# Mixture-of-experts stage of a two-layer hybrid step: the raw weight ring turns unbroken over the fixed rounds, the 64-slot tile's down product moves behind its next gate product, and the 128-slot rounds split their weights one unit further ahead

## The reference

```python
N_EXP = 8
TOP_K = 2
D_FF_E = 1408

def moe_swiglu(h, router, w_gu, w_down):
    ...
    logits = (hf @ router).astype(jnp.float32)
    top_v, top_i = lax.top_k(logits, TOP_K)
    wts = jax.nn.softmax(top_v, axis=-1)
    ...
    g, u = jnp.split(jnp.einsum('nd,edf->nef', hf, w_gu), 2, axis=-1)
    act = jax.nn.silu(g) * u * gate[..., None].astype(h.dtype)
    return jnp.einsum('nef,efd->nd', act, w_down).reshape(B, T, D)
```

## Time and profile before

| | before |
|---|---|
| time, median of 3 runs | 2532.23 us (2530.74 to 2536.68) |
| the profiled execution's own time | 2524.19 us |
| its span, first to last instruction | 2522.5 us |
| PE busy | 2192.5 us, 87% of the span |
| DVE busy | 1326.5 us, 53% |
| ACT busy | 935.1 us, 37% |
| HBM traffic | 134 GB/s over the span |

### The profile page before, as it was taken

One profiled execution on the slowest core, in us unless ns is written; L12 is line 12 of the kernel. 1 busy time (PEld: TensorE's weight loads), 2 busy tenths in 40 slices (PEclk: granted clock), 3 DMA queues, 4 the chain that ended last, 5 costly groups with the idle time before them and its releaser, 6 DMA issues. The chain is left out here.

```text
span 2522.5 us, 41799 instructions
## 1 busy us (share of the span) xinstructions
PE 2192.5 (87%) x17111; PEld 1845.0 (73%) x17111; DVE 1326.5 (53%) x1865; ACT 935.1 (37%) x1462; POOL 425.2 (17%) x459
## 2 busy tenths in 40 slices
PE   5998597999899999998994878988699898899993
PEld 4987365668899999998983665677467666787882
DVE  5566666654422222235565676644355655655546
ACT  4333024653422112114331246633344544544443
POOL 0036332541000000000064334610100000000002
PEclk8999798999899999998997899999799999999996
DMA  6331773923222232212315710021766877846645
GB/s 225 87 93 34 168 239 107 343 88 101 62 73 63 80 83 68 58 52 66 89 30 122 196 62 1 1 65 44 272 208 210 291 242 255 283 158 225 217 147 193
DMA packets 370847, 340.75 MB, mean 135 GB/s; under 512 B 90593, under 2 KB 339887, under 8 KB 369647
## 3 DMA queue, kind: packets, MB, share of 16 engines
q1 hardware_dynamic: 354447, 279.26, 36.4%
q10 hardware_dynamic: 11520, 41.95, 5.1%
q0 software_dynamic: 4704, 17.04, 1.7%
HBM read 287.42 MB, written 50.79 MB: 134 GB/s over the span
## 5 line engine op out<-in xcount | busy, mean ns | idle before, releaser
L2839 DVE TENSOR_TENSOR w_lo<-w_raw,w_hi 128x2048 fp32r<-128x2048 f32 (+1 forms) x138 | 306.5, 2228 | 156.8 <-ACT w_hi L2677 156.4
L2677 ACT CAST w_hi<-w_raw 128x2048 fp32r<-128x2048 f32 (+1 forms) x138 | 255.0, 1856 | 47.9 <-PE ps L2609 29.3
L2577 PE MATMUL ps<-w_hi,h_hi 128*128 128x512 f32 (+1 forms) x528 | 203.5, 385 | 20.6 <-DVE w_lo L2839 20.6
L2577 PE MATMUL ps<-w_hi,h_lo 128*128 128x512 f32 (+1 forms) x528 | 198.2, 375 | 0.0
L2577 PE MATMUL ps<-w_lo,h_hi 128*128 128x512 f32 (+1 forms) x528 | 198.1, 375 | 0.0
L3121 PE MATMUL ps<-ffn_h_hi,w_hi_ffn 128*128 128x320 f32 x704 | 161.5, 311 | 5.5 <-DVE ffn_h_lo L379 4.2
L3121 PE MATMUL ps<-ffn_h_lo,w_hi_ffn 128*128 128x320 f32 x704 | 161.3, 310 | 0.0
L3121 PE MATMUL ps<-ffn_h_hi,w_lo_ffn 128*128 128x320 f32 x704 | 161.3, 310 | 0.0
L1869 DVE TENSOR_REDUCE tm<-ps 128x1 f32<-128x768 f32 (+1 forms) x140 | 111.7, 818 | 49.7 <-PE ps L1765 31.6
L2577 PEld LDWEIGHTS ps<-w_hi,h_hi 128*128 128x128 f32 x528 | 100.4, 190 | 49.8 <-issue 22.6
L571 PE MATMUL ps<-w_hi_in,h_hi 128*128 128x454 f32 x320 | 122.4, 382 | 4.8 <-DVE w_lo_in L153 3.3
(11 more groups left out here) (478 smaller groups left out, 5155.1 us busy)
## 6 DMA issues: line engine op xcount, KB each, us to landing
w_raw<-in_moe_w_gu SPq DMA_DIRECT2D x186, 512.0 KB, 5.1
w_raw<-in_moe_w_down SPq DMA_DIRECT2D x41, 1024.0 KB, 7.3
G_decay<-in_ada_w ACTq DMA_DIRECT2D x54, 512.0 KB, 4.6
w_ahead<-in_ffn_w_gu SPq DMA_DIRECT2D x44, 512.0 KB, 5.3
slots_h<-tm SPq DMA_DIRECT2D x14, 1024.0 KB, 10.7
slots_y<-tm SPq DMA_DIRECT2D x13, 1024.0 KB, 11.6
w_ahead<-in_ffn_w_down SPq DMA_DIRECT2D x16, 704.0 KB, 4.7
oA<-in_ada_w ACTq DMA_DIRECT2D x20, 512.0 KB, 4.8
```

Source lines behind the costliest of these rows:

```text
L2577: mm = pe.matmul(ps[:, bank, 0:2 * columns(u)], x[:, k, tile * P:(tile + 1) * P], gate_up(wt, u, k), start=(k == 0 and n == 0), stop=(k == ...
L2677: act.copy(part(whi, n), raw_piece(n)).then_inc(s["w_hi"], 1)
L2839: dve.tensor_tensor(part(wlo, n), raw_piece(n), part(whi, n).bitcast(F32), ALU.subtract).then_inc(s["w_lo"], 1)
```

## The change

Three things are altered, all of them in the rounds.

1. **Places in the ring.** Over the fixed rounds, a piece's place is its number counted from the first round, modulo 6, and no longer from the start of its own round. With 17 pieces a round, before, the first pieces of the next round waited for pieces 12 to 16 and 11; now they wait for 11 to 16 in turn. In the loop the turn is still broken at each round (`holder`, `raw_slot`, `landed`).
2. **The small tile's down product.** Unit u-1's is now issued right behind unit u's small gate product. It raises a semaphore of its own, `few_dn`, which SP waits for; `dn` is raised by tile 0's down product. The last unit's goes in the order small tile, then tile 0.
3. **Splits in 128 rounds.** The two gate pieces of unit 1 are split at the start of the round, and behind the `gate` of unit u both gate pieces of unit u+2; `take` follows, then the split of d(u). Piece d5 is split after the last of these. The loads' order is unchanged.

```diff
-        raw_slot = [n % RAW for n in range(NP)]
...
+        loop_slot = [(NP * STATIC + n) % RAW for n in range(NP)]
...
+            def splits_of(c):
+
+                if c != 128:
+                    return list(range(NP))
+                order_ = [at("g", 0, 0), at("g", 0, 1), at("g", 1, 0), at("g", 1, 1)]
+                for u in range(NU - 1):
+                    order_ += next_pieces(u)
+                    order_ += [at("d", u, 0)]
+                order_ += [at("d", NU - 1, 0)]
+                return order_
...
+            def holder(r, n, ahead):
+
+                if not ahead:
+                    return n - RAW
+                if isinstance(r, int):
+                    return NP + n - RAW
+                return max(m for m in range(NP) if loop_slot[m] == loop_slot[n])
...
                     def down(r, u, tile):
                         c = size(r)
                         pe.wait_ge(s["a_lo"], unit_done(r, u))
-                        pe.wait_ge(s["w_lo"], count("pieces", r, at("d", u) + 1))
+                        pe.wait_ge(s["w_lo"], rank(r, at("d", u)))
...
-                        if tile == max(tiles_of(c)):
+                        if few(c, tile):
+                            mm.then_inc(s["few_dn"], 1)
+                        elif tile == (0 if c == 192 else max(tiles_of(c))):
                             mm.then_inc(s["dn"], 1)
...
                             for tile in order:
                                 multiply(r, u, tile)
+                                if u and few(c, tile):
+                                    down(r, u - 1, tile)
...
-                            if u and c == 192:
-                                down(r, u - 1, 1)
-                        for tile in range(len(order)):
+                        for tile in order:
                             down(r, NU - 1, tile)
...
+                        if c == 128:
+                            split(r, at("g", 1, 0))
+                            split(r, at("g", 1, 1))
                         for u in range(NU - 1):
                             gate(r, u, order[0])
+                            if c == 128:
+                                for n in next_pieces(u):
+                                    split(r, n)
+                                take(r, u, 0)
+                                split(r, at("d", u))
+                                continue
                             split(r, 3 * u + 2)
...
+                        if c == 128:
+                            split(r, at("d", NU - 1))
                         gate(r, NU - 1, order[0])
                         split(r, 0, 1)
```

More of the change, by code:

```diff
@@ L2276, in experts @@
             names = (self.NORM + " w_in io zeroed moved_pool mm_t lg_t mm chain diff expd chosen count turned_t h_tok slots table scattered issued "
-                     "blk_in h_turned h_hi h_lo w_hi w_lo gu silu prod a_turned a_hi a_lo dn y_act y_dve y_store y_free "
+                     "blk_in h_turned h_hi h_lo w_hi w_lo gu silu prod a_turned a_hi a_lo dn few_dn y_act y_dve y_store y_free "
                      + " ".join(f"raw{q}" for q in range(RAW)))
@@ L2418, in wait_raw_free @@
             def wait_raw_free(eng, r, n):
[L2420 to L2425, removed]
+                kind, u, _ = ORDER[n]
+                eng.wait_ge(s["w_hi"], rank(r, n))
+                eng.wait_ge(s["w_lo"], rank(r, n))
+                if size(r) == 192:
                     if kind == "g":
-                        eng.wait_ge(s["gu"], tile_count(r - 1 if n < 0 else r, u, 1))
+                        eng.wait_ge(s["gu"], tile_count(r, u, 1))
                     else:
-                        eng.wait_ge(s["dn"], count("units", r - 1 if n < 0 else r, u + 1))
+                        eng.wait_ge(s["few_dn"], count("few", r, u + 1))
             with stage(nc, names) as (block, s):
@@ L2673, in split @@
                     def split(r, n, ahead=0):
[L2674 to L2675 removed]
+                        act.wait_ge(s[f"raw{raw_slot(r, n, ahead)}"], landed(r, n, ahead))
                         wait_used(act, r, hl_before[n] + NP * ahead)
[L2677 removed]
+                        act.copy(part(whi, n), raw_piece(r, n, ahead)).then_inc(s["w_hi"], 1)
                     def gate(r, u, tile):
@@ L2837, in split @@
                     def split(r, n, ahead=0):
-                        dve.wait_ge(s["w_hi"], count("pieces", r, NP * ahead + n + 1))
-                        dve.tensor_tensor(part(wlo, n), raw_piece(n), part(whi, n).bitcast(F32), ALU.subtract).then_inc(s["w_lo"], 1)
+                        dve.wait_ge(s["w_hi"], rank(r, n, ahead))
+                        dve.tensor_tensor(part(wlo, n), raw_piece(r, n, ahead), part(whi, n).bitcast(F32), ALU.subtract).then_inc(s["w_lo"], 1)
                     def gate(r, u, tile):
@@ L2941, in _ @@
                     for q in range(RAW):
-                        pool.wait_ge(s[f"raw{q}"], per_round[q] * rounds + (per_round[q] * STATIC + landed[q]))
+                        pool.wait_ge(s[f"raw{q}"], loop_total[q] * rounds + (static_total[q] + incs[loop_slot.index(q)]))
     def combine(self, l, pos, w):
```

74 lines of the change are left out of this document (46 added, 28 removed).

## The result

The changed kernel took 2545.94 us in the median of 5 runs (2541.0 to 2556.53), the kernel before 2532.23 (2525.2 to 2536.68). The ratio is 1.0074, with a 95% interval of 1.0052 to 1.0095: slower by 13 to 24 us, where 7.5 was forecast. The direction was right, the size was not. The time itself lies in the range of 2529 to 2550.

The account below looks back on a forecast made before the run. PE bounds the 192 rounds; 128 rounds, where PE waits mostly for DVE's w_lo, have something to give. 22.5 us lost less 15 gained is 7.5 slower: 2532.23 + 7.5 = 2539.7 us, range 2529 to 2550 (8 in 10).

Parts of the forecast that it names:

- What bounds the kernel: Fixed rounds: PE busy 79.7 of 82 us in a 192 round, 52 to 53 of 66 to 67 in a 128 round.
- the 256 rounds at nothing: 256 rounds: they keep their order and ring, so their cost was put at zero.
- PE stands longer in the 192 rounds: 192 rounds: new waits at the moved small down product, for w_lo or a_lo, lose 7.0 + 7.75 + 7.75 = 22.5 us.
- PE stands less in the 128 rounds: 128 rounds: earlier splits shorten PE's waits, giving 3.7 us in round three and 3.4 in round five.
- the clock: 128 rounds and behind round three: with no wait over 2.4 us left, the clock stays up, giving 2.6 + 1.7 + 1.6 us.
- the rest: 128 rounds: 0.6 us each from gate products no longer standing still midway, and the gain of 14.2 rounded up to 15.
- the bound of 27: 192 rounds: upper bound of the loss in three rounds, 3 x 9 us; the lower bound was nothing.
- the part on the loads: 128 rounds: at 352 GB/s g31 lands at about 19 us, wanted at 16.2, which takes 1.5 us back.
- the sign of being wrong: 128 rounds: waits of ACT for DMA of more than 3 us would say that the loads bind.
- Faster as a rival: 128 rounds run at PE's pace alone, giving 34 us, less 22.5 lost in the 192 rounds: 2521 us; chance 0.15.
- The rival of over 11 us slower: Waits of 2.0 to 2.5 us in 192 and 128 rounds each halve the clock, 1.7 us each time: 2551; chance 0.16.
- The ring does nothing as a rival: Ring: loads had slack, so its turn gives nothing; inside the forecast, 1 to 3 us of the gain; no chance given.

Follow-up runs that it names:

- e3: Changed kernel, small down product waiting only for its raw piece and its own tile's activation; ratio 0.9966 to the kernel before.
- e9: Changed kernel, next round's block loaded behind the round's first four weight loads; 128 rounds 64.9 and 62.0 us, in the changed kernel 63.7 each.
- e12: Changed kernel, small down product waiting for the raw piece instead of w_lo, still for both tiles' activations; 192 rounds 85.1 and 86.7 us.
- e8: e3 with the splits of 128 rounds half a unit ahead, in the loads' order; ratio 0.9875 to the kernel before, 128 rounds 54.4 and 55.5 us.
- e5: Kernel before with the ring's unbroken turn alone (dn and few_dn apart, old place); 128 rounds 67.1 and 67.2 us, before 67.3 and 66.2.
- e1: Changed kernel with the small down product back in its old place; ratio 0.9961 to the kernel before, 128 rounds 64.7 and 65.5 us.
- e6: Kernel before with the earlier splits alone (dn and few_dn apart, old place, old ring); 128 rounds 68.5 and 67.9 us, before 67.3 and 66.2.
- e2: Kernel before with only the small down product moved (dn and few_dn apart); ratio 1.0110 to the kernel before, 192 rounds 92.4 and 92.6 us.
- e4: Changed kernel loading half of each gate piece and each down piece but the last in 128 rounds; these took 59.7 and 60.7 us.
- e10: e8 with the small down product in its old place; ratio 0.9891 to the kernel before, 128 rounds 56.2 and 55.5 us.

## Why the prediction was off

**What bounds the kernel, and the 256 rounds at nothing:** right.

**The sum, term by term.** The same terms, counted in the two traces over the five fixed rounds. PE's standing time is a round's length less PE's busy time. The clock's cost is my estimate, half of the time for which PE was busy at the lower of the two levels, 1.2 GHz: 12.3 us in these rounds before and 22.3 in the changed kernel.

| | forecast | measured |
|---|---|---|
| PE stands longer in the 192 rounds | 22.5 | 6.8 + 7.6 + 7.5 = 21.9 |
| PE stands less in the 128 rounds | -3.7 - 3.4 = -7.1 | -2.1 - 4.3 = -6.4 |
| the clock | -2.6 - 1.7 - 1.6 = -5.9 | 11.2 - 6.2 = +5.0 |
| the rest | -0.6 - 0.6 - 0.8 = -2.0 | -0.3 |
| sum | 7.5 | 20.2 |

So the step that failed is the one on the clock: "I take these as given back, as no wait over 2.4 us is left in a 128 round". The clock was to give 5.9 us and cost 5.0 (1.7 of it at the start of the first round, see below), which is 10.9 of the 12.7 us that the forecast is off.

**The 192 rounds:** the mechanism was as forecast. The single waits were forecast as 2.0, three of 1.1, 2.5 and 1.5 (1.0 in the first round), and came as 1.9, 1.1, 1.1, 0.6, 2.6 and 1.4 (0.6). The 0.6 is unit 4, where the transposes of the next block stand between and cover; I had overlooked them there. A unit took 15.4 us, for 15.2 in the forecast. The rounds lost 26.3 us, though the third had a slow start before, of 1.5 us, that was gone; the sum counts it with the clock. With it the loss is 27.8, just over the bound of 27. What was missing is the clock: I had priced waits of 2.5 us at no fall, and in the second 192 round it fell behind the 2.6 us wait. The first began at a low clock, at some 1.7 us (its first 32 matmuls took 5.36 us instead of 3.67). I don't put that down to the change, as e3, e9 and e12, which are the same up to there, began at the full clock.

**The 128 rounds:** they gave 6.1 us in the two themselves. The granted clock was 0.95 in the first, as before, and 0.92 in the second, where it had been 0.97. The premise of the clock step failed in two ways. First, a wait over 2.4 us was left, and this is in the part on the loads. It says that the lead leaves only g31 late, at a price of 1.5 us. I had not held the first piece that is asked for earlier, g21, against its own landing. By the same numbers it could be seen: g20, the block, the store and g21 are 3.7 MB, 10.4 us at 352 GB/s, and ACT was to want it at about 8. Counted from the round's first matmul, it wanted it at 7.8 and had it at 11.6. So unit 1's down product waited 4.6 and 3.8 us where the forecast had 1.2, and the clock fell at both. ACT's waits of 3.9 and 4.6 us for this piece are the sign of being wrong that the prediction names, over 3 us. Second, shorter waits lowered the clock as well: in the second 128 round it fell behind 2.39 and 1.81 us, two of the waits behind which the prediction says that it stays up.

That the waits of the 128 rounds nearly add up is luck. The other waits were 2.4 for 2.2 at the first transpose, 1.8 for 1.8 in unit 5, and 2.1 and 0.4 for 2.4 at the end; unit 2, forecast at 0.8 and 1.5 for g31, made nothing, and unit 3, forecast at 0.4, made 1.0. The long wait ahead took the place of the later ones. With the clock, chance plays a part in these sizes too, since there is one profile of each kernel.

**Faster as a rival** counted on PE's pace in the 128 rounds, 34 us. The changed kernel did not come near it. e8 got 23.6 of these 34 us: not by splitting a whole unit earlier, but by splitting in the order in which the pieces land and are used.

**The rival of over 11 us slower**, at a chance of 0.16, is what happened, in size and in mechanism: it has waits of 2 to 2.5 us that lower the clock, and 18.5 us slower. Not all falls were where it had them: of the six, two came at the waits for g21, one behind a wait of 1.8 us and one at the start of the first round. The page of the Trainium skill that I set against the trace ("TensorE: Matmul & The Clock Gate", A second HAM failure mode) came closer than I gave it credit for: the clock fell behind waits as short as 1.8 us, though not behind all of them.

**The ring does nothing as a rival:** the ring alone gave nothing (e5), but with the earlier splits it was worth 3.8 + 2.4 us, which is e1 against e6.

## What to carry to other kernels

When a consumer is moved closer to its producer, list all that its wait stands for and ask which of it the consumer reads: a shared wait (`w_lo`, both tiles) that was free at the old place cost 7 to 10 us a round at the new one, and e3 took it back by waiting for what is read. When a gain is counted on a clock that stays up, ask for each wait that is left what rows of the same length show. When work is pulled ahead, check the first piece that it now asks for, not the last, with all bytes that share the way; of the leads tried, half a unit, in the order of the loads, was the best. Compare stages, not spans, where an untouched stage ahead moves by 18 us from profile to profile.

## What the runs showed of the hardware

A wait of PE of the same length does not always lower the clock. The wait of 2.59 us ahead of unit 5's small down product stands in 15 rounds of five kernels (the changed one, e2, e4, e9, e12). In 6 of them the clock stayed at the full level; in 9 it fell to half within 1 us of the start of the product that follows. Falls stand behind shorter waits too: the wait of 1.8 us ahead of unit 5's down product stands in 14 of the 128 rounds (of the changed kernel, e1, e3, e4, e6, e9 and e12), and in 6 of them the clock fell within 1.4 us behind it. A fall cost about 1.7 us, as the two 192 rounds of e12 show, 85.1 and 86.7 us, which have the same waits. A window in unit 5 of each, with the fall and without:

```profile
2106.00:2112.00 6.00, 5.07 (x21) 2.31 (x22) 4.34 (x5) 1.34 (x1) 0.00 (x0) 0.72 0.62 187
1958.00:1964.00 6.00, 5.67 (x38) 4.04 (x39) 4.03 (x5) 1.37 (x3) 0.00 (x0) 1.00 0.80 276
```

The DMA kept 360 and 363 GB/s over the 54 and 55 us of e8's 128 rounds, and 366 and 369 over those of e10, above the 352 of the busiest 44 us before, with the share of busy time at 1.07 in all four. So the 352 that the prediction calls all that it gave was not its limit.
